# A decoder layer on one Trainium2 core: the routing products read column blocks of the rows, most of them issued inside the last output product

## What is computed

```python
x = x + merged @ w_o[l]
x = x + hierarchical_moe(rmsnorm(x, g_ffn[l]), w_route_group[l], ...)
...
g_logits = (xf @ w_rg) + b_rg            # 4 groups
e_logits = (xf @ w_re) + b_re            # 32 experts; top group, then the top 2 of its 8 experts
...
return (jax.nn.silu(xb @ w1[e]) * (xb @ w3[e])) @ w2[e]
...
return rmsnorm(x, g_final)
```

## Time and profile before

| what | value |
|---|---|
| median of 3 runs | 723.98 us (723.43 to 724.48) |
| profiled execution, its own time | 723.45 us |
| its span, first to last instruction | 721.7 us |
| TensorE busy | 684.8 us, 95% |
| VectorE, ScalarE, GpSimd busy | 245.8, 192.3 and 4.2 us |
| memory traffic | 243.73 MB, 338 GB/s over the span |

### The profile page before, as it was taken

How to read it: one execution, slowest core, us unless ns; L and a number is a source line. 1 busy time by engine, 2 the same in 40 slices (tenths; PEclk the granted TensorE clock), 3 DMA queues, 4 the chain that set the end, 5 groups by cost and what they waited for, 6 DMA issues and landing times.

```text
span 721.7 us, 10098 instructions
## 1 busy us (share of the span) xinstructions
PE 684.8 (95%) x4067; PEld 406.5 (56%) x4067; DVE 245.8 (34%) x524; ACT 192.3 (27%) x304; POOL 4.2 (1%) x8
## 2 busy tenths in 40 slices
PE   4999999999999999999999999799999898998995
PEld 4999977777777874444344344344444343453432
DVE  6643466666667764121111111021111020111112
ACT  5542455589654431010100100010110010000112
POOL 0100000000000000000000000000000000000000
PEclk9999999999999999999999999999999999999999
DMA  8998541356347987999999999999999999999993
GB/s 308 302 340 232 167 127 59 117 196 213 133 158 287 400 362 250 403 429 426 427 424 430 423 427 426 425 424 430 426 427 424 429 426 428 426 427 425 418 399 112
DMA packets 45063, 243.73 MB, mean 338 GB/s; under 512 B 10144, under 2 KB 12376, under 8 KB 32728
## 3 DMA queue, kind: packets, MB, share of 16 engines
q1 hardware_dynamic: 44568, 241.45, 83.8%
q0 software_dynamic: 448, 1.59, 0.6%
HBM read 241.96 MB, written 1.07 MB: 337 GB/s over the span
## 4 chain that ended last, share of the span: by engine, by line
PE 71%; DMA 15%; SPq 5%; DVE 4%; issue 2%; ACT 2%; POOLq 0%; DVEq 0%; ACTq 0%
PE bank L1674 24%; DMA unit<-in_w 14%; PE bank L1729 9%; PE bank L1361 8%; PE bank L1362 8%; PE bank L1363 8%; SPq L536 5%; PE bank L1652 4%; PE bank L1741 2%; PE bank L1742 1%; DMA unit<-in_w_in 1%; DVE low L327 1%; PE bank L1703 1%; PE bank L1439 1%; PE bank L1684 1%
## 5 line engine op out<-in xcount | busy, mean ns | idle before, releaser
L1674 PE MATMUL bank<-unit,xT 128*64 128x512 f32 x1024 | 230.5, 602 | 14.4 <-DMA unit<-in_w 9.1
L1674 PEld LDWEIGHTS bank<-unit,xT 128*64 128x64 f32 x1024 | 76.7, 138 | 152.7 <-issue 147.5
L1729 PE MATMUL bank<-unit,hidT 128*64 128x512 f32 x480 | 106.3, 596 | 0.0
L1361 PE MATMUL bank<-high,hT_hi 128*128 128x512 f32 (+2 forms) x224 | 83.3, 372 | 1.3 <-DVE low L327 1.3
L1362 PE MATMUL bank<-low,hT_hi 128*128 128x512 f32 (+2 forms) x224 | 81.0, 362 | 0.0
L327 DVE TENSOR_TENSOR low<-unit,high 128x2048 fp32r<-128x2048 f32 (+1 forms) x34 | 70.7, 2098 | 9.5 <-ACT high L322 9.5
L1363 PE MATMUL bank<-high,hT_lo 128*128 128x512 f32 (+2 forms) x192 | 68.6, 357 | 0.0
L1729 PEld LDWEIGHTS bank<-unit,hidT 128*64 128x64 f32 x480 | 33.2, 137 | 61.5 <-issue 59.9
L322 ACT ACTIVATE high<-unit 128x2048 fp32r<-128x2048 f32 (+1 forms) x34 | 58.9, 1756 | 13.0 <-PE bank L1363 10.1
L1248 DVE TENSOR_TENSOR y_lo<-bank,y_hi 128x512 fp32r<-128x512 f32 x30 | 20.7, 691 | 94.1 <-ACT y_hi L782 94.1
L1652 PEld LDWEIGHTS bank<-pick,hk 128*128 128x128 bf16 x768 | 44.4, 98 | 13.5 <-issue 12.2
(11 more groups left out here) (241 smaller groups left out, 685.3 us busy)
## 6 DMA issues: line engine op xcount, KB each, us to landing
unit<-in_w SPq DMA_DIRECT2D x86, 2048.0 KB, 29.0
unit<-in_w_gate SPq DMA_DIRECT2D x8, 2048.0 KB, 9.9
unit<-in_w SPq DMA_DIRECT2D x12, 1024.0 KB, 28.0
unit<-in_w SPq DMA_DIRECT2D x14, 512.0 KB, 8.4
unit<-in_w_in SPq DMA_DIRECT2D x3, 2048.0 KB, 14.6
unit<-in_w_in SPq DMA_DIRECT2D x4, 1024.0 KB, 11.1
unit<-in_w_br SPq DMA_DIRECT2D x4, 1024.0 KB, 5.2
unit<-in_w_o SPq DMA_DIRECT2D x2, 2048.0 KB, 10.2
```

Of the source, the lines that this page charges most:

```text
L1361: mm(dst, a_hi, b_hi, start=first, stop=False)
L1674: last = mm(bank[4 + w][g * CAP:(g + 1) * CAP, :], xT[:, k, g * CAP:(g + 1) * CAP], rhs, start=(k == 0), stop=(k == KD - 1))
L1729: last = mm(bank[6 + n][g * CAP:(g + 1) * CAP, :], hidT[:, c, g * CAP:(g + 1) * CAP], rhs[:, c, n * BANK:(n + 1) * BANK], start=(c == 0), ...
```

## The change

The routing transposes take blocks of 128 neighbouring columns (`turn_rows`), so a half of a row (t, i) needs only `add_product(t, i)`; `wr` and a second copy of `g_ffn` (`gffn_rows`, loaded by a new transfer) lie in memory to match. Three of the four halves are turned and multiplied by `wr` inside product (1,1). `h2T` becomes two tiles, one over `hT_hi` and one over `wo_lo`, of which each uses the token columns that its product no longer needs. Two of the three early `absorb` stand behind product (1,1), around the last `turn_rows`; the third after the last `route`; the small fills are 40 in place of 20. The last quarter's `remain` moves from VectorE to GpSimd, and ScalarE makes that quarter's squares and root ahead of its `first_part`. The subtraction of 1 from `slot` is dropped, and `slot_no` is raised by 1 ahead of time instead.

```diff
--- before.py
+++ after.py
@@ -66,6 +66,7 @@
 QUARTERS = ((0, 0), (1, 0), (0, 1), (1, 1))
+TURNED = {q: i + 1 for i, q in enumerate(QUARTERS)}
@@ -131,6 +132,7 @@
         nsink = place("nsink", [P, 4])
+        gffn_rows = place("gffn_rows", [P, KD])
         assert at[0] <= after_pad, (at[0], after_pad)
@@ -145,7 +147,6 @@
         hT_hi = place("hT_hi", [P, KD, TOK], F32R)
-        h2T = place("h2T", [P, KD, TOK], offset=hT_at)
         xT = place("xT", [P, KD, P], offset=hT_at)
@@ -182,6 +183,8 @@
         wo_lo = place("wo_lo", [P, KD, TOK], F32R, offset=shared)
+        h2T = [place(f"h2T{t}", [P, KD, TOK], offset=(hT_at, shared)[t]) for t in range(NT)]
         sig_at = at[0]
@@ -235,7 +238,7 @@
         gate3 = place("gate3", [P, NT, NE, 3], BF16)
-        lg = place("lg", [P, NT, NG + NE])
+        lg = place("lg", [P, NT, NG + NE], offset=pad)
         ge = place("ge", [P, NT, NG])
@@ -406,8 +409,9 @@
                 sp.dma_start(gffn[:], a["g_ffn"][0].rearrange("(p k) -> p k", k=KD)).then_inc(s["wr"], 16)
-                sp.dma_start(wr[:, :, 0:NG], a["w_route_group"][0].rearrange("(p k) n -> p k n", k=KD)).then_inc(s["wr"], 16)
-                sp.dma_start(wr[:, :, NG:], a["w_route_expert"][0].rearrange("(p k) n -> p k n", k=KD)).then_inc(s["wr"], 16)
+                sp.dma_start(gffn_rows[:], a["g_ffn"][0].rearrange("(k p) -> p k", k=KD), allow_slow_non_contiguous=True).then_inc(s["wr"], 16)
+                sp.dma_start(wr[:, :, 0:NG], a["w_route_group"][0].rearrange("(k p) n -> p k n", k=KD)).then_inc(s["wr"], 16)
+                sp.dma_start(wr[:, :, NG:], a["w_route_expert"][0].rearrange("(k p) n -> p k n", k=KD)).then_inc(s["wr"], 16)
                 sp.dma_start(rbias[:, 0:NG], a["b_route_group"][0].partition_broadcast(P)).then_inc(s["wr"], 16)
@@ -564,6 +568,11 @@
             pool.dma_start(bias_d[:], bass.AP(dram_vec.tensor, 8 * MAP, [[1, P], [MAP, 4], [1, TOK]])).then_inc(s["biasT"], 16)
+            t, cols, qs = quarter(3)
+            pool.wait_ge(s["parts1"], 4)
+            pool.wait_ge(s["parts3"], 2)
+            nc.gpsimd.tensor_tensor(remainder[1][:], x[:, t, cols].rearrange("p (q k) -> p k q", k=KD), hk_1[:, t, :, qs],
+                                    ALU.subtract).then_inc(s["remains"], 1)
             pool.wait_ge(s["xg"], 1)
@@ -751,9 +760,9 @@
             second_part(2)
-            first_part(3)
             row_squares(3)
             second_norm(1)
+            first_part(3)
             second_part(3)
@@ -1082,7 +1091,7 @@
-            dve.wait_ge(s["wr"], 16 * 5)
+            dve.wait_ge(s["wr"], 16 * 6)
             def add_product(t, n):
@@ -1106,15 +1115,22 @@
-                dve.wait_ge(s["h2ps"], 2 * t + i + 1)
+                dve.wait_ge(s["h2ps"], TURNED[t, i])
                 ks = slice(4 * i, 4 * i + 4)
-                V.tensor_tensor(h2T[:, ks, t * P:(t + 1) * P], bank[2 * t + i][:].rearrange("p (k t) -> p k t", k=4),
-                                gffn[:, ks].unsqueeze(2).broadcast_to([P, 4, P]), ALU.mult).then_inc(s["h2T"], 1)
+                V.tensor_tensor(h2T[t][:, ks, 0:P], bank[2 * t + i][:].rearrange("p (k t) -> p k t", k=4),
+                                gffn_rows[:, ks].unsqueeze(2).broadcast_to([P, 4, P]), ALU.mult).then_inc(s["h2T"], 1)
...
                 V.reciprocal(rs[:, t:t + 1], rs[:, t:t + 1]).then_inc(s["rs"], 1)
+            def logits(t):
+                dve.wait_ge(s["lg_ps"], t + 1)
+                dve.wait_ge(s["rs"], t + 1)
+                return V.scalar_tensor_tensor(out=lg[:, t, :], in0=bank[4 + t][:, 0:NG + NE], scalar=rs[:, t:t + 1],
+                                              in1=rbias[:], op0=ALU.mult, op1=ALU.add)
@@ -1125,31 +1141,26 @@
             link(V.tensor_copy(ident_bf[:], ident))
+            link(V.tensor_scalar(slot_no, slot_no, 1.0, None, ALU.add))
             second = cst[:, C_GE + CAP:C_GE + CAP + 1].unsqueeze(1).broadcast_to([P, NT, 3])
...
             add_product(0, 1).then_inc(s["x1"], 1)
+            weighted_turned(0, 0)
+            weighted_turned(1, 0)
             second_norm(0)
             remain(2)
-            weighted_turned(0, 0)
             weighted_turned(0, 1)
...
             add_product(1, 1).then_inc(s["x1"], 1)
-            weighted_turned(1, 0)
             weighted_turned(1, 1)
-            remain(3)
             second_norm(1)
+            link(logits(0))
+            link(logits(1))
...
             from_end = lambda n: cst[:, C_IOTA:C_IOTA + n].unsqueeze(1).broadcast_to([P, NT, n])
-            R = NG + NE
-            for t in range(NT):
-                dve.wait_ge(s["lg_ps"], t + 1)
-                dve.wait_ge(s["rs"], t + 1)
-                link(V.scalar_tensor_tensor(out=lg[:, t, :], in0=bank[4 + t][:, 0:R], scalar=rs[:, t:t + 1],
-                                            in1=rbias[:], op0=ALU.mult, op1=ALU.add))
             link(V.tensor_reduce(m[:, 0, :], lg[:, :, 0:NG], AX, ALU.max))
@@ -1181,7 +1192,6 @@
                                         scalar=1.0, in1=asg[:], op0=ALU.add, op1=ALU.mult))
-            link(V.tensor_scalar(slot[:], slot[:], -1.0, None, ALU.add))
@@ -1569,13 +1579,20 @@
-            def turn_tile(t, rows, done):
+            def turn_tile(t):
...
                     for kk in range(4):
-                        k_th = rows[:, t, :].rearrange("p (q k) -> p k q", k=KD)[:, 4 * i + kk, :]
+                        k_th = merged[:, t, :].rearrange("p (q k) -> p k q", k=KD)[:, 4 * i + kk, :]
                         last = nc.tensor.transpose(bank[2 * t + i][:, kk * P:(kk + 1) * P], k_th, ident)
-                    last.then_inc(done, 1)
+                    last.then_inc(s["mTps"], 1)
+            def turn_rows(t, i):
+                pe.wait_ge(s["x1"], TURNED[t, i])
+                for k in range(4 * i, 4 * i + 4):
+                    last = nc.tensor.transpose(bank[2 * t + i][:, (k % 4) * P:(k % 4 + 1) * P], x[:, t, k * P:(k + 1) * P], ident)
+                last.then_inc(s["h2ps"], 1)
@@ -1588,13 +1605,13 @@
                     last.then_inc(s["wo"], 1)
-                elif (t, n) == (1, 1):
+                elif (t, n) == (1, 1) and ks[-1] == 3:
                     last.then_inc(s["wo_rows"], 1)
...
-            def route(t, ks=range(KD)):
+            def route(t, ks):
                 for k in ks:
-                    pe.wait_ge(s["h2T"], 2 * t + k // 4 + 1)
-                    last = mm(bank[4 + t][:, 0:NG + NE], h2T[:, k, t * P:(t + 1) * P], wr[:, k, :],
+                    pe.wait_ge(s["h2T"], TURNED[t, k // 4])
+                    last = mm(bank[4 + t][:, 0:NG + NE], h2T[t][:, k, 0:P], wr[:, k, :],
                               start=(k == 0), stop=(k == KD - 1))
@@ -1603,35 +1620,37 @@
             pe.wait_ge(s["mrg"], 14)
-            turn_tile(0, merged, s["mTps"])
+            turn_tile(0)
             branch(3, 3)
...
             pe.wait_ge(s["mrg"], 16)
-            turn_tile(1, merged, s["mTps"])
+            turn_tile(1)
             out_product(0, 0, range(4, KD))
...
             out_product(0, 1)
+            turn_rows(0, 0)
+            turn_rows(1, 0)
             out_product(1, 1, range(4))
-            pe.wait_ge(s["x1"], 3)
-            turn_tile(0, x, s["h2ps"])
-            out_product(1, 1, range(4, KD))
+            turn_rows(0, 1)
             route(0, range(4))
-            pe.wait_ge(s["x1"], 4)
-            turn_tile(1, x, s["h2ps"])
+            route(1, range(4))
+            out_product(1, 1, range(4, 6))
             route(0, range(4, KD))
-            route(1)
+            out_product(1, 1, range(6, KD))
...
+            absorb(0, 0)
+            turn_rows(1, 1)
+            absorb(1, 0)
+            route(1, range(4, KD))
+            absorb(0, 1)
             pe.wait_ge(s["bf"], 2)
-            for t, n in ((0, 0), (0, 1), (1, 0)):
-                absorb(t, n)
-            for _ in range(20):
+            for _ in range(40):
                 mm(bank[7][:, 0:P], ones_bf[:], before_bf[:], start=True, stop=True)
```

## The result

The changed kernel takes 724.91 us (median of 20 runs, 722.67 to 727.09) beside 723.49 us (20 runs, 721.06 to 724.89) for the kernel before on the same chip: ratio 1.0020, 95% interval 1.0012 to 1.0028. That is slower by 1.4 us, where I had forecast 2.7.

The account below looks back on a forecast made before the run. The prediction took the weight transfers to bound 286 to 704 us, so the end follows the first expert product's start. Order +1.5 and hold +1.2 gave +2.7 us, a forecast median of 726.7 us, range 723.9 to 728.5.

Parts of the forecast that it names:

- Four transposes and twelve routing steps in the product: On TensorE ahead of the last matmul of product (1,1): they release that matmul 3.05 us later.
- The shorter tail behind it: From the last matmul of (1,1) to the second logits instruction: 3.32 us instead of 4.64, so -1.32.
- The dropped subtraction: Subtraction of 1 leaves the chain to the first expert product: -0.23 us; the addition replacing it costs nothing.
- the order: Rearranged work up to the first expert product: +3.05 - 1.32 - 0.23 = +1.5 us.
- rival (c): Rows put into product (1,1) hide beside its matmuls; only the shorter tail counts: -1.55, 722.4 us; chance 0.15.
- the hold: After the logits, VectorE's two-input instruction `ge` waits until GpSimd's subtraction ends: +1.2 us.
- my lower bound of 1.57: Shortest duration expected for GpSimd's subtraction, from its one multiplication of the same 128 x 512; 2.0 us was taken.
- the estimate of 2.1 us: GpSimd's subtraction by the engine reference: 1.96 times VectorE's 1.08 us.
- The third and 40 fills take 3.6 us, under the 4.8 ... no cost.: Third absorption plus fills on TensorE fit between the logits and the last third part behind `asg`, costing nothing.
- So the end of the kernel moves one for one with the moment at which that product starts.: A microsecond won or lost before the first expert product, at 272.07 us, is a microsecond of the whole.
- rival (d): No change: slack further on in the weight stream takes up the late start; 724.0 us; chance 0.10.
- rival (b): No hold: GpSimd and VectorE run side by side after the logits; +1.5, 725.5 us; chance 0.28.

Follow-up runs that it names:

- fills_60: The changed kernel with 60 small fills instead of 40; 723.61 us.
- routing_as_fill: The changed kernel with all routing steps moved back behind product (1,1) and the absorptions behind them; 721.46 us, ratio 0.9972 to the kernel before.
- fills_80: The changed kernel with 80 small fills instead of 40; 725.04 us.
- after_again: The changed kernel, unedited, run for a second profile and more runs; 724.94 us.
- after_front_20: The changed kernel with 40 semaphore waits, which make 20 instructions, added at the head of TensorE's part; 725.46 us.
- before_fills_40: The kernel before with 40 small fills instead of 20; 721.13 us.
- before_middle_40: The kernel before with 40 semaphore instructions added between its fills and the wait on `asg`; 724.85 us.
- routing_fills_20: The routing_as_fill kernel with 20 small fills instead of 40; 722.78 us.
- before_front_40: The kernel before with 40 semaphore instructions added at the head of TensorE's part, no product more; 719.48 us.
- remain_on_vector: The changed kernel with the last subtraction back on VectorE, between its two logits instructions; 724.95 us.
- pool_twice: The changed kernel with GpSimd's last subtraction done twice, once into a tile nobody reads; 726.43 us (one run).

## Why the prediction was wrong, step by step

**Right.** Four transposes and twelve routing steps in the product cost 3.08 us (forecast 3.05). The shorter tail behind it gave 1.24 (forecast 1.32). The dropped subtraction is worth 0.23 (from the counting products to the gather 1.35 us in fills_60, 1.58 before, both at full clock). That is +1.6 us from the order, and rival (c), that they hide in the product, is refuted: routing_as_fill has the same rows behind the product and is 3.58 us shorter in the stretch, of which 1.38 is clock and 0.28 hold.

**Mis-sized: the hold.** The mechanism I took was the right one, but it cost 0.28 us instead of 1.2. GpSimd's duration was 1.41 us, below my lower bound of 1.57: its row of one multiplication was no bound from below, and the estimate of 2.1 us was too high as well. Of the 0.9 too much, 0.6 is this duration, 0.2 its start, 0.49 us ahead of the logits instead of 0.28, and 0.15 that `ge`'s own time lies within the hold and not behind it.

**Wrong: "The third and 40 fills take 3.6 us, under the 4.8 ... no cost."** I asked only whether the fills would be too long. They were too short: the absorptions that had covered the wait for `asg` were moved forward, the fills end 2.00 us before the counting products, and the clock halves for the absorption (1,1) and the gather. That is 0.95 for the one and 0.53 for the other here, less 0.1 of waits, 1.38 in all: fills_60 and fills_80 take it away. The row that should have warned me is the absorptions' own, 3.9 us for four: what TensorE did ahead of a wait was taken away, and I gave it no price as cover. Even so my own numbers left a hole of about 1.3 us (4.8 less 3.6, and the 0.09 from the last routing step to the logits), near the 1.13 at which the clock stays up. It became 2.00 because the hold put off `asg` by 0.28 and the absorption and 40 fills, begun 0.27 ahead of the logits, took 3.34 us instead of 3.6.

**Wrong: "So the end of the kernel moves one for one with the moment at which that product starts."** It does where TensorE's program ahead of the experts' loop is as long as it was, or long enough. Without a wait on issue in either, routing_as_fill is 3.6 us shorter in the stretch than after_again and 3.5 faster, fills_60 is 1.4 shorter than after_front_20 and 1.9 faster, before_fills_40 is 3.3 shorter than before_middle_40 and 4.0 faster. So a reserve in the weight stream that takes up a late start, rival (d), is refuted. But the edit also lengthened the program ahead of the loop, and I gave that no term. In time, at the same stretch, it is worth 2.0 us by before_fills_40 and 1.3 by routing_fills_20; before_middle_40, 3.28 us longer in the stretch, lost 2.0 us of time, so it got 1.3 back. before_front_40 shows 3.4 (722.84 and 719.48), but with the gain at the head of the program in it, and its interval (1.9 to 4.1 us) overlaps that of before_fills_40 (1.1 to 3.0).

Put together: +3.26 us in the stretch (order +1.61, hold +0.28, clock +1.38, within 0.01) less 1.3 to 2.0 for the program's length gives +1.3 to +2.0; measured was +1.4. The forecast of +2.7 missed a loss of 1.4 and a gain of about 1.8, beside 0.9 too much for the hold. That the kernel came out slower by an amount inside my range is therefore partly luck: the loss by the clock and the gain in the experts' part, neither of them foreseen, nearly cancel. By its number rival (b), +1.5, comes nearest, and that is luck too, since the hold that it denies is there.

**Not settled.** Why a longer program ahead of the loop saves time. In the changed kernel the gain is found in the experts' part, 1.94 and 1.69 us shorter in two pairs of profiles. It goes with the lost wait on issue, but not with its size: with the wait the part is 431.85 to 432.14 us (four profiles of three kernels), without it 430.05 to 431.59, so at the nearest 0.3 us apart (routing_fills_20 and routing_as_fill). Nor does the wait leave a gap in the transfers that bound this part: from 440 to 520 us the DMA share of the kernel before is 0.98 to 1.04 in every 4 us. In before_fills_40 and before_front_40 the profiles show only 0.7 and 1.5 us less in the experts' part; another 2.4 and 2.7 us they gained in the first 22 us, where TensorE's products grow short sooner. (These products start 0.21 us apart at first and then 0.12, nearly the ratio of the two clock levels, but the profile's granted clock reads 1.00 there throughout, so that this is the clock is not shown.) before_fills_40 has no edit there, and the two profiles of the changed kernel differ by 1.7 us in the same way, so for it this can be the chance of one execution; how much of it is in the medians no run tells. That the wait is one for instructions to be fetched is argued from the packets of the instruction queue (10 against 2 or 3 from 400 to 550 us, in every kernel with and without it) and not shown.

## What to carry to other kernels

Price what an instruction does as cover before you move it away from a wait: a hole of 2 us ahead of a short chain of products can cost more in clock than the instruction did, and a few neutral products fill it. Check both ends of such a fill, that it isn't too long and that it isn't too short. Where a loop's first turns show a wait on issue, compare the number of instruction packets between kernels, and before you believe a change of 0.2 or 0.3%, shift the loop by some tens of neutral instructions and time that as well. Then look at the start of the trace, too: neutral instructions at the head of a queue can change when its first work begins.

## What the runs showed of the hardware

- TensorE's clock fell to 0.50 after holes of 2.00 us (changed), 2.24 (remain_on_vector), 3.18 (pool_twice) and 3.28 us (before_middle_40), and stayed at 1.00 after holes of 1.13 us (before) and 0.90 us (fills_60). An absorption takes 1.89 us at the lower level and 0.95 at the full one.
- Forty semaphore instructions on TensorE, all met, took 3.28 us, 0.08 each; forty products of 128 columns took 2.40.
- GpSimd's subtraction of 128 x 512 with a strided input took 1.41 us, 1.3 times VectorE's 1.08; its multiplication with one input takes 1.57.
- The point at which TensorE's products of 256 columns fall from 0.41 to 0.28 us at the start of the program varies from 15.3 to 17.8 us between two profiles of one kernel, and the start of product (1,1) with it by 1.7 us.
- Twenty fills ahead of the experts' loop, forty instructions, made the kernel before 2.0 us of 723 faster with its stretch unchanged.
